# Modulation weights by 64 rows: a vector's two parts on 64 partitions each, summed by pairs of matmuls over 64 partitions

## What is computed

```python
def ada_modulation(c, ada_w, ada_b):          # c 1x1024, ada_w 1024x6144, ada_b 6144
    m = jax.nn.silu(c) @ ada_w + ada_b
    return jnp.split(m, N_MOD, axis=-1)

def even_layer(x, c, ada_w, ada_b, ...):
    sh_m, sc_m, g_m, sh_f, sc_f, g_f = ada_modulation(c, ada_w, ada_b)
    h = modulate(rms_norm_2(x, mix_norm), sh_m, sc_m)
    ...
    x = x + g_m[:, None, :] * y
    hf = modulate(rms_norm_2(x, ffn_norm), sh_f, sc_f)
    return x + g_f[:, None, :] * swiglu(hf, ffn_w_gate, ffn_w_up, ffn_w_down)
```

## Time and profile before

| | us |
|---|---|
| median of 3 runs | 901.8 (901.21 to 901.86) |
| the profiled execution | 901.51 |
| its span | 899.4 |

### The profile page before, as it was taken

How to read it: one execution, slowest core, us unless ns; L and a number is a source line. 1 busy time by engine, 2 the same in 40 slices (tenths; PEclk the granted TensorE clock), 3 DMA queues, 4 the chain that set the end, 5 groups by cost and what they waited for, 6 DMA issues and landing times.

```text
span 899.4 us, 13652 instructions
## 1 busy us (share of the span) xinstructions
PE 888.7 (99%) x5057; PEld 761.6 (85%) x5057; DVE 695.0 (77%) x723; ACT 487.3 (54%) x651; POOL 29.3 (3%) x52
## 2 busy tenths in 40 slices
PE   8999999999999999999999999999999999999998
PEld 5998879999999699979888888878777888888886
DVE  5698978988888887996888888687796775655655
ACT  5545574444445758755455455455675465545542
POOL 4000100000000000011000000010000100000000
PEclk9999999999999999999999999999999999999999
DMA  6989586999898385556988887636434365555561
GB/s 217 341 276 340 175 293 208 365 358 320 333 326 316 102 277 170 181 165 201 360 304 318 318 297 280 189 98 211 137 115 142 117 209 190 187 187 186 187 188 69
DMA packets 117093, 208.08 MB, mean 231 GB/s; under 512 B 7236, under 2 KB 81068, under 8 KB 111928
## 3 DMA queue, kind: packets, MB, share of 16 engines
q1 hardware_dynamic: 116566, 205.31, 66.8%
q10 hardware_dynamic: 290, 2.10, 0.7%
q0 software_dynamic: 192, 0.05, 0.0%
HBM read 206.39 MB, written 1.05 MB: 231 GB/s over the span
## 4 chain that ended last, share of the span: by engine, by line
PE 94%; ACT 2%; DVE 2%; DMA 1%; issue 0%; SPq 0%; DVEq 0%; ACTq 0%
PE tp L1891 8%; PE ub L1891 8%; PE acc L1796 7%; PE acc L1797 7%; PE acc L1799 7%; PE acc L1744 5%; PE acc L1746 5%; PE acc L1745 5%; PE tp L1892 4%; PE ub L1892 4%; PE tp L1909 4%; PE acc L1909 4%; PE ub L1880 3%; PE ub L1879 3%; PE ub L1878 3%; PE acc L1878 3%
## 5 line engine op out<-in xcount | busy, mean ns | idle before, releaser
L1124 DVE TENSOR_TENSOR w_lo<-w_raw,w_hi 128x1024 fp32r<-128x1024 f32 x288 | 348.7, 1221 | 115.1 <-ACT w_hi L700 114.4
L700 ACT ACTIVATE w_hi<-w_raw 128x1024 fp32r<-128x1024 f32 x288 | 302.3, 1058 | 241.8 <-PE acc L1799 71.0
L1891 PE MATMUL tp<-aT,w_hi 128*128 128x512 f32 x320 | 114.1, 399 | 0.0
L1891 PE MATMUL ub<-aT,w_hi 128*128 128x512 f32 x320 | 113.8, 398 | 0.0
L1796 PE MATMUL acc<-w_hi,hT_hi 128*128 128x512 f32 x288 | 112.8, 392 | 0.1
L1797 PE MATMUL acc<-w_lo,hT_hi 128*128 128x512 f32 x288 | 112.2, 390 | 0.0
L1799 PE MATMUL acc<-w_hi,hT_lo 128*128 128x512 f32 x272 | 106.1, 390 | 0.0
L1892 PE MATMUL tp<-aT,w_lo 128*128 128x256 f32 x320 | 89.9, 281 | 0.0
L1892 PE MATMUL ub<-aT,w_lo 128*128 128x256 f32 x320 | 89.8, 281 | 0.0
L1891 PEld LDWEIGHTS tp<-aT,w_hi 128*128 128x128 f32 x320 | 60.1, 188 | 14.9
L1891 PEld LDWEIGHTS ub<-aT,w_hi 128*128 128x128 f32 x320 | 60.1, 188 | 14.6
(11 more groups left out here) (282 smaller groups left out, 1526.8 us busy)
## 6 DMA issues: line engine op xcount, KB each, us to landing
ada_raw<-in_l_ada_w SPq DMA_DIRECT2D x24, 1024.0 KB, 6.0
w_raw<-in_l_ffn_w_gate SPq DMA_DIRECT2D x44, 512.0 KB, 4.6
w_raw<-in_l_ffn_w_up SPq DMA_DIRECT2D x44, 512.0 KB, 3.8
w_raw<-in_l_ffn_w_down SPq DMA_DIRECT2D x44, 512.0 KB, 3.4
w_raw<-in_w_up SPq DMA_DIRECT2D x32, 512.0 KB, 4.5
w_raw<-in_w_down SPq DMA_DIRECT2D x32, 512.0 KB, 5.2
scratch<-in_l_ada_w SPq DMA_DIRECT2D x14, 1024.0 KB, 7.7
w_raw<-in_attn_w_qkv SPq DMA_DIRECT2D x24, 512.0 KB, 6.3
```

Source lines behind the costliest of these rows:

```text
L700: act.activation(w_hi[:, v % SLOTS, :], w_raw[:, v % SLOTS, :], ACT.Copy).then_inc(hi_done, 1)
L1124: dve.tensor_tensor(w_lo[:, n, :], w_raw[:, n, :], w_hi[:, n, :].bitcast(F32), ALU.subtract).then_inc(lo_done, 1)
L1891: pe.matmul(banks[f], w_hi[:, v % SLOTS, c], aT[:, :, b, :], start=b == 0, stop=False)
```

## The change

The modulation weights, all but layer 1's first third, are no longer loaded by blocks of 128 rows. A block is now of 64 rows, and its vectors of 1024 columns are cut in two: the first 512 columns of each vector lie on partitions 0 to 63, the second 512 on partitions 64 to 127. A slot holds the same bytes as before. Since one DMA can't write this layout, there are two for each block, of 64 partitions each, with runs of 2 KB (before: one DMA with 8 KB, or 4 KB in the attention, a partition). `silu_c` gets further columns, silu(c) by groups of 64 on both halves of the partitions, from two more small loads and one more transpose at step X.

DVE's steps keep their number and size: 128 partitions by 4 times 512 columns, or by 2 times 512. The gathered values of a vector are 512 columns wide, in the place of its first half in `mod`.

A sum is now over 64 partitions, and the two sums of a vector are a pair: two fp32 matmuls over different halves of the partitions into two banks (`ada_pair`). Ten pairs take the place of twenty sums, the four rounded ones among them; `rounded_sums`, the steps X0 and X1, and the rounding on ACT and DVE are gone. Since the first half of a vector is written where the gathered values lie, ACT's copies wait for both sums of a pair, and sums always come in pairs, where before one stood alone (three and one become two and two).

Around that: at the entry of `w_qkv` ACT copies the sums before it rounds the weight part, and DVE's gate of the second tile is cut in two with the first tile's rows between the halves. Before the odd layer's SwiGLU the last pair goes to two banks of `acc` once x is final, and DVE's rows wait for the copy of each half that they need, not for both.

```diff
-LRU_STEPS = steps("""... L6 M7 X0 U5 H7 S0 F0 X1 G1 D0 E2
+LRU_STEPS = steps("""... L6 M7 U5 H7 S0 F0 G1 D0 E2
...
-        silu_c = sb("silu_c", [P, KB])
+        silu_c = sb("silu_c", [P, 3 * KB])
...
+        def raw_halves(v0, v1):
+
+            return mod[:, v0 * D:v1 * D].rearrange("p (v h n) -> p v h n", h=2, n=CH)[:, :, 0, :]
...
+            if m >= 22:
+                return acc[:, 2 + m % 2, :]
             return (tp if m < 12 else ub)[:, m % 2, :]
...
+        ada_w_halves = [a[f"l{n}_ada_w_2"].rearrange("(k q) (v h n) -> q k h v n", q=HP, h=2, n=CH) for n in (0, 1)]
...
-                layer, third = cols_of
-                src = ada_w[layer][:, bass.ds(rb, 1), third * UNIT:(third + 1) * UNIT]
-                sp.dma_start(ada_slot[slot].unsqueeze(1), src).then_inc(ada_loaded[slot], 16)
+                for n in range(2):
+                    src = ada_w_halves[layer][:, bass.ds(rb, 1), n, 2:6, :]
+                    sp.dma_start(by_vector(ada_slot[slot][side(n), :]).unsqueeze(1), src).then_inc(ada_loaded[slot], 16)
...
-                sp.dma_start(mix_slot[n % 6], ada_w[0][:, n // 2, n % 2 * D:(n % 2 + 1) * D]).then_inc(mix_loaded[n % 6], 16)
+                for h in range(2):
+                    sp.dma_start(by_vector(mix_slot[n % 6][side(h), :]),
+                                 ada_w_halves[0][:, n, h, 0:2, :]).then_inc(mix_loaded[n % 6], 16)
...
                     row_square(t, x[:, t, :])
+                    if t == 0 or k == 4:
+                        ada_parts(layer, parts[1 + t], parts[2 + t])
                     if k == 4:
                         split_part(2 * u + 2 + t)
-                    if t == 0 or k == 4:
-                        ada_parts(layer, parts[1 + t], parts[2 + t])
...
-                    act.wait_ge(ada_sum, 12 * layer + n + 1)
+                    act.wait_ge(ada_sum, 12 * layer + (n + 1 if layer and c < 4 else n // 2 * 2 + 2))
...
                 for g in range(2):
+                    if out:
+                        dve.wait_ge(ada_out, out + g + 1)
...
-                gate(1, g_mod)
+                gate(1, g_mod, 0)
                 norm_rows(0, g, shift)
+                gate(1, g_mod, 1)
                 add_gated(1).then_inc(x_ready, 1)
...
-                if n >= 2:
-                    dve.wait_ge(mix_used, n - 1)
-                part = mod[:, n % 2 * D:(n % 2 + 1) * D]
-                dve.scalar_tensor_tensor(part, mix_slot[n % 6], silu_c[:, n // 2:n // 2 + 1], part,
+                if n >= 1:
+                    dve.wait_ge(mix_used, n)
+                raw = raw_halves(0, 2)
+                dve.scalar_tensor_tensor(raw, by_vector(mix_slot[n % 6]), silu_c[:, KB + n:KB + n + 1], raw,
                                          ALU.mult, ALU.add).then_inc(mix_used, 1)
...
+            def ada_pair(layer, n):
+
+                c, m = ADA_ORDER[layer][n], 12 * layer + n
+                if 8 <= m < 22:
+                    pe.wait_ge(ada_out, m)
                 for i in range(2):
-                    hi, lo = (part[i] for part in halves)
-                    out = sum_bank(m + i) if len(hi.shape) == 2 else blocks_of_bank(sum_bank(m + i), hi.shape[-1])
-                    pe.matmul(out, ones_r[:, :], hi, start=True, stop=False)
-                    pe.matmul(out, ones_r[:, :], lo, start=False, stop=True).then_inc(ada_sum, 1)
...
+                    pe.matmul(sum_bank(m + i), ones[side(i), :], mod[side(i), c * CH:(c + 1) * CH], start=True,
                               stop=True).then_inc(ada_sum, 1)
...
-            ada_sums(0, 0, 3)
-            entry(U_MLP, tp_banks, before_T1=lambda: ada_sums(0, 3, 4), tile1_out=1)
+            ada_pair(0, 0)
+            entry(U_MLP, tp_banks, before_T1=lambda: ada_pair(0, 2), tile1_out=1)
...
-            ada_sums(1, 8, 12)
+            ada_pair(1, 8)
+            pe.wait_ge(x_ready, 10)
+            ada_pair(1, 10)
             swiglu(1)
```

More of the change, by code:

```diff
@@ L39 @@
 HALF = 256
+HP = P // 2
 UNIT = 2048
@@ L183, in block_program, with side, by_vector @@
         c_rows = scratch[0:KB, 8192 + LRU:8192 + LRU + P]
+        c_half_rows = scratch[0:2 * KB, 8192 + LRU + P:8192 + LRU + 2 * P]
+        def side(n):
+            return slice(n * HP, (n + 1) * HP)
+        def raw_halves(v0, v1):
+            return mod[:, v0 * D:v1 * D].rearrange("p (v h n) -> p v h n", h=2, n=CH)[:, :, 0, :]
+        def by_vector(slot):
+            return slot.rearrange("p (v n) -> p v n", n=CH)
         xn_flat = xn[:, :, :].rearrange("p t n -> p (t n)")
@@ L490, in _ @@
                        (c_rows[:, :], a["c_2"].rearrange("a (k p) -> (a k) p", p=P))]
+            for n in range(2):
+                vectors.append((c_half_rows[:, side(n)], a["c_2"].rearrange("a (k q) -> (a k) q", q=HP)))
             for dst, src in vectors:
@@ L655, in _ @@
             for step, n in ATT_STEPS:
-                if step == "E" and n < 3:
-                    start_sums(0, n)
+                if step == "E" and n < 2:
+                    start_sums(0, (0, 2)[n], (2, 6)[n])
             pool.wait_ge(o_ready, HEADS)
             pool.wait_ge(mix_used, 11)
-            start_sums(1, 0, mod_next)
+            start_first()
             half_var(0, 0)
@@ L804, in _ @@
             first_norm(U_QKV1)
-            act.activation(ones_r[:, :], ones[:, :], ACT.Copy)
-            def rounded(dst, src):
-                act.activation(dst[0], src, ACT.Copy).then_inc(ada_hi, 1)
             for step, n in ATT_STEPS:
```

140 lines of the change are left out of this document (61 added, 79 removed).

## The result

| | median, us | range | against before |
|---|---|---|---|
| before | 901.64 | 901.21 to 901.86 | |
| changed | 980.96 | 968.4 to 994.8 | 1.079, 95% interval 1.070 to 1.088 |

The change makes the kernel 79 us slower, 8.8%, by the medians; the ratio in the table is that of the fast runs alone (968.4, 969.5 and 980.4 us), which lie 71 us above the kernel before, while the profiled execution, 994.8 us, is a slow one. What follows reads places and rates in it. Where a size matters, the trace of a later experiment with the same kind of loads, 975.43 us in all, is set beside it.

A forecast was written before the change was run, and what follows sets the result against it. PE, busy 99% of the span, was taken to bound the kernel, DMA nearly as full. Terms 0.26 + 0.3 + 0.7 - 0.85 - 0.75 + 0.1 + 0.2 = 0.0 gave 901.5 us; 8-in-10 range 899.4 to 935.

The forecast's parts named there:

- I take the lower end: Modulation-weight loads: a load of 64 partitions costs nothing more than its shorter runs; bounds up to +2.77 us a megabyte.
- rival 1: Halves load at half rate in MLP, SwiGLU and attention: +57, 958 us, or 912 if loads behind fill in; chance 0.31.
- The pairs: Sums on PE: two 64-partition sums run side by side, 0.86 us plus about 0.4 for edges, 1.27 us standing alone.
- Both tiles: Before tile 1 at the MLP and w_in, a pair replaces one sum: +0.26 and +0.3 us.
- LRU: Steps S0 and S1: each pair of rounded sums goes from 0.92 to 1.27 us, together +0.7 us.
- PE would stand still for what it saves: Entries of the MLP and w_in: three sums become a pair, but the transposes wait for xn anyway, so 0.
- The entry of `w_qkv`: Copies go ahead of ACT's weight rounding; transposes begin 1.1 us earlier, net -0.85 us (bounds -1.1 and -0.3).
- PE needs that part later still: Entry of w_qkv: ACT's rounding of the weight part comes 1.1 us later, but PE needs it later than that.
- The gate: Entry of w_qkv: only half of DVE's gate stands ahead of the rows, 0.6 us less, xn ready near 589.4.
- The odd SwiGLU's entry: Rows need only sum 21 and transposes start at about 706.9 instead of 707.67: -0.75 us (bounds -1.0 and 0).
- Shorter runs: Loads in 2 KB runs: +0.8 us a slice, hidden in the loops (0); +0.2 us in attention (bounds 0 and +2).
- Rivals 2, 3 and 4: Faster, no edges, full entries: 899.4 us, 0.13; pairs not side by side: 906 us, 0.04; front slips 2 us: 903.5 us, 0.07.

The follow-up runs named there:

- the second experiment: The kernel before, with each modulation-weight load cut in two of 64 partitions, runs, sums and order untouched: 985.56 us (975.43 to 995.3), 1.097.
- the second of these kernels: The changed kernel with 128-partition loads (other rows land) and, at the entry of w_qkv, the second tile's gate in one piece ahead of the rows: 903.43 us.

## Why the prediction was wrong

- **The step that failed** is "I take the lower end" for a load of 64 partitions. I had its bounds (0 to +2.77 us a megabyte), in rival 1 the rule of the Trainium skill with its rates ("SBUF — State Buffer", "Door 1: The DMA port swizzle (why [64,N] ≈ [32,N])", 196 against 328 GB/s), and stretches at a DMA share of 0.84 to 1.00, and took zero because engines and bytes stay the same. They did. What fell is the rate at a full share: 218 to 220 GB/s for halves, 369 to 399 for whole blocks, 2.0 to 2.5 us a megabyte. With no row of a large one, the only stated rate was the better evidence, and by my own account anything from 0.8 us a megabyte on would show.
- **Rival 1 was right in kind and too small**: the range ended at 935 because I cut rival 1 in the middle, between 912, where loads behind fill half of the lost time, and its full price of 958. The result lies above even that, by 10 us in the fastest execution. Attention: +11 forecast, 17 measured. MLP: +24, and 33 in the changed kernel's trace, 20 in that of the second experiment. SwiGLU: +22, and 41 or 36. The price a megabyte (2.77) was rather too high (2.0 to 2.5). What is too small is the cover: I set 1.6 us a slice in the MLP, 2.7 in the SwiGLU and half of attention's 22 us against it, and 40 MB at 2.0 to 2.5 us with no cover at all (80 to 100 us) is nearer to what was measured (67 to 93). Why the cover was not there stays open. Slots that came back later are one reading; PE's clock is another, with 25 us more of busy time though there are fewer sums, of which no run shows how much the whole paid for.
- **The pairs** were right: side by side, with all edges, 1.26 for 1.27 us. Both tiles and LRU came within about 0.1 us. (1.27 less 0.92 is 0.35, not the 0.33 of my sum.)
- **"PE would stand still for what it saves"**, so 0, was wrong at `w_in`: the wait grew from 0.20 to 1.72 us and cost 1.0 us of products in one trace, 2.9 in another, through the clock, and nothing in three executions whose clock stayed at 1.00.
- **The entry of `w_qkv`**: the transposes were right (-1.03 for -1.1). "PE needs that part later still" was the step that failed; PE stood 1.39 us for it, and the entry cost 0.4 us where I had -0.85. The gate, which I counted as a gain, was none.
- **The odd SwiGLU's entry**: -0.74 for -0.75, as forecast, of which 0.18 is lost again behind it.
- **Shorter runs**: 0 in the loops was right (1.0002), +0.2 in the attention too small to be seen. **Rivals 2, 3 and 4** did not come.

## What to carry to other kernels

A load that fills partitions 0 to 63 or 64 to 127 took 1.6 to 1.8 times the time for the same bytes here, and it took it from all loads behind it in a full queue. Look at the DMA share first: where it is as high as here (0.84 to 1.00), keep every large load at 128 partitions and at an outermost step of many, even where the arithmetic would like another layout. Time saved in front of a wait is not free: ask what fills PE there, because after a stop the clock of the work behind it may be half. And of an instruction that is moved ahead, name the one that it is moved ahead of and who waits for that.

## What was not expected of the hardware

- Two queues that write the two sides at once took 29.6 us for what one queue took 40.7, alone; with weight loads between them little of the gain was left (18.2 against 18.7 us a round).
- A load whose outermost step is of two ran on two of the 16 engines: 51 GB/s, share 0.13.
- The slow level of the clock after the same stop of PE lasted for a different time from trace to trace, +1.0 us of products in one and +2.9 in the next, and three executions of the second of these kernels show none of it (901.9 to 902.5 us, mean clock 1.00).
